# Whole-row pieces of the expert weights, and both column halves of a matrix accumulated together

## The reference

```
logits = x @ w_router + b_router;  top 4 of 32 experts, softmax over the 4
for each expert e, rows xb that chose it:
    gate = min(xb @ w_gate[e] + b_gate[e], 7)
    up   = clip(xb @ w_up[e] + b_up[e], -7, 7)
    glu  = gate * sigmoid(1.702 * gate)
    out  = ((up + 1) * glu) @ w_down[e] + b_down[e]
y[token] += weight * out
```

## Time and profile before

| what | value |
|---|---|
| time, median of 3 runs | 2386.68 us (2386.51, 2386.68, 2390.77) |
| profiled execution, first to last instruction | 2388.7 us (no other time of its own is given) |
| TensorE busy | 2262.0 us, 95% |
| VectorE busy | 1463.2 us, 61% |
| ScalarE busy | 1098.7 us, 46% |
| DMA | 493.68 MB, 207 GB/s over the span |

### The profile page before, as it was taken

How to read it: one execution, slowest core, us unless ns; L and a number is a source line. 1 busy time by engine, 2 the same in 40 slices (tenths; PEclk the granted TensorE clock), 3 DMA queues, 4 the chain that set the end, 5 groups by cost and what they waited for, 6 DMA issues and landing times. The chain is left out here.

```text
span 2388.7 us, 28681 instructions
## 1 busy us (share of the span) xinstructions
PE 2262.0 (95%) x10214; PEld 1643.8 (69%) x10215; DVE 1463.2 (61%) x1924; ACT 1098.7 (46%) x1057; POOL 89.8 (4%) x182
## 2 busy tenths in 40 slices
PE   7988999997799879999999999999999999999996
PEld 2765737774467567777777777777777777777774
DVE  1345222424100157878788888878887878788773
ACT  2241121201110037657676675765775656566552
POOL 0211202002000000000000000000000000000000
PEclk9899999986799959999999999999999999999998
DMA  8251251201524328778788787877886778678640
GB/s 307 77 176 37 71 210 71 80 1 36 196 80 141 121 78 294 263 259 300 280 298 303 267 315 277 298 247 281 291 318 234 268 251 307 228 283 315 228 158 24
DMA packets 262257, 493.68 MB, mean 207 GB/s; under 512 B 9883, under 2 KB 27484, under 8 KB 262151
## 3 DMA queue, kind: packets, MB, share of 16 engines
q1 hardware_dynamic: 260362, 490.69, 58.0%
q10 hardware_dynamic: 1840, 2.25, 0.3%
HBM read 486.47 MB, written 6.43 MB: 206 GB/s over the span
## 5 line engine op out<-in xcount | busy, mean ns | idle before, releaser
L1784 DVE TENSOR_TENSOR low<-ring,high 128x2048 fp32r<-128x2048 f32 x384 | 865.1, 2287 | 129.3 <-ACT high L1589 129.3
L1589 ACT ACTIVATE high<-ring 128x2048 fp32r<-128x2048 f32 x384 | 732.5, 1921 | 195.5 <-PE ps_moe L1666 125.6
L1663 PE MATMUL ps_moe<-high,xh 128*128 128x512 f32 x1024 | 414.2, 404 | 2.2 <-DVE xh L1789 2.2
L1666 PE MATMUL ps_moe<-low,xh 128*128 128x512 f32 x1024 | 400.8, 391 | 0.0
L1648 PE MATMUL ps_moe<-pick,work 128*128 128x128 f32 (+1 forms) x1584 | 285.4, 311 | 3.1 <-DVE pick L1751 3.1
L724 PE MATMUL ps_mix<-hT,ring 128*128 128x320 f32 x896 | 265.1, 453 | 16.0 <-ACT cbuf L641 6.7
L1648 PEld LDWEIGHTS ps_moe<-pick,work 128*128 128x128 f32 (+1 forms) x1584 | 221.1, 193 | 65.0 <-issue 3.8
L724 PEld LDWEIGHTS ps_mix<-hT,ring 128*128 128x128 f32 x896 | 175.8, 199 | 92.8 <-issue 18.3
L1663 PEld LDWEIGHTS ps_moe<-high,xh 128*128 128x128 f32 x1024 | 193.2, 189 | 57.1 <-issue 18.4
L1666 PEld LDWEIGHTS ps_moe<-low,xh 128*128 128x128 f32 x1024 | 193.5, 189 | 37.7
L1663 PE MATMUL ps_moe<-high,hh 128*128 128x512 f32 x512 | 206.7, 404 | 0.0
(11 more groups left out here) (354 smaller groups left out, 2111.9 us busy)
## 6 DMA issues: line engine op xcount, KB each, us to landing
ring<-in_w_gate SPq DMA_DIRECT2D x128, 1024.0 KB, 7.3
ring<-in_w_up SPq DMA_DIRECT2D x128, 1024.0 KB, 5.1
ring<-in_w_down SPq DMA_DIRECT2D x128, 1024.0 KB, 6.5
ring<-in_w_in SPq DMA_DIRECT2D x18, 2048.0 KB, 7.9
ring<-in_w_ada SPq DMA_DIRECT2D x12, 2048.0 KB, 8.1
states<-in_state_gdn_rec SPq DMA_DIRECT2D x8, 512.0 KB, 8.2
out_rec_sample<-states SPq DMA_DIRECT2D x8, 512.0 KB, 3.2
ring<-in_w_branch_b SPq DMA_DIRECT2D x2, 2048.0 KB, 15.8
```

The costliest lines, as they stand in the source:

```text
L1589: nc.scalar.activation(r(high[:, p % SPLIT]), raw_piece(ring, p), ACT.Copy).then_inc(high_s, 1)
L1663: nc.tensor.matmul(ps[:, bank, :], r(high_x[:, c, :]), r(hb[:, k, :]), start=c == 0, stop=False)
L1666: last = nc.tensor.matmul(ps[:, bank, :], r(high_x[:, c, :]), r(lb[:, k, :]), start=False, stop=False)
L1784: nc.vector.tensor_tensor(r(low[:, p % SPLIT]), raw_piece(ring, p), high[:, p % SPLIT], ALU.subtract).then_inc(low_s, 1)
```

## The change

A piece is now 256 whole rows of a matrix, and a partition gets two neighbouring rows, 2048 floats that lie together. A piece therefore holds two row chunks for both column halves: the even rows of the 256 and the odd ones. `half` becomes `matrix`, which accumulates both column halves in two banks, goes through four pieces, and ends with two bias matmuls in a row. Because row chunk c is now every second row, the stationary operands of `gather` and `fold_half` are read with a step of two elements (`pair_rows`), so that x and hid have their rows in the same order. TensorE's order becomes matrix 0, matrix 1, then fold (0,0), (0,1), combine 0, fold (1,0), combine 1, fold (1,1), gather, matrix 2. ScalarE and VectorE are put in a new order to match; the numbers and sizes of their instructions stay.

```diff
-            name, a, q = ("w_gate", "w_up", "w_down")[p // 4], p // 2 % 2, p % 2
-            src = t[name][0, e, QUART * P * q:QUART * P * (q + 1), HALF * a:HALF * a + HALF].rearrange("(c p) n -> p c n", p=P)
-            sp.dma_start(raw_piece(ring, p), src).then_inc(raw_full[p % RAW], 16)
+            name, q = ("w_gate", "w_up", "w_down")[p // 4], p % 4
+            src = t[name][0, e, 2 * P * q:2 * P * (q + 1), :].rearrange("(p c) n -> p (c n)", c=2)
+            sp.dma_start(raw_piece(ring, p).rearrange("p c n -> p (c n)"), src).then_inc(raw_full[p % RAW], 16)
...
ScalarE:
-                    act.wait_ge(piece_t, PIECES * i + 4 * m + 2 * a + 2)
+                    act.wait_ge(piece_t, PIECES * i + 4 * m + 4)
...
-                for p in range(3, 6):
+                for p in range(3, 7):
                     round_piece(p)
                 rows_out(0, 0)
-                for p in range(6, 8):
-                    round_piece(p)
                 rows_out(0, 1)
-                for p in range(8, 10):
+                for p in range(7, 11):
                     round_piece(p)
                 rows_out(1, 0)
...               (the two sigmoids)
-                for p in range(10, 12):
-                    round_piece(p)
                 rows_out(1, 1)
+                round_piece(11)
...
TensorE:
-                                                h2tok[0:n, tau, P * c:P * c + P], pick[0:n, tau, :],
+                                                h2tok[0:n, tau, pair_rows(c)], pick[0:n, tau, :],
...
+            def matrix(i, m, high_x, low_x, wide):
                 rows = slice(64, 128) if m == 1 else slice(0, 64)
+                for q in range(4):
+                    p = 4 * m + q
+                    pe.wait_ge(low_s, PIECES * i + p + 1)
+                    hb, lb = (x[:, p % SPLIT].rearrange("p k n -> p (k n)") for x in (high, low))
+                    for kk in range(2):
+                        c = 2 * q + kk
+                        for a in range(2):
+                            cols = slice(D * kk + HALF * a, D * kk + HALF * a + HALF)
+                            out = ps[:, 2 * m + a, :]
+                            nc.tensor.matmul(out, r(high_x[:, c, :]), r(hb[:, cols]), start=c == 0, stop=False)
+                            if wide:
+                                nc.tensor.matmul(out, r(low_x[:, c, :]), r(hb[:, cols]), start=False, stop=False)
+                            last = nc.tensor.matmul(out, r(high_x[:, c, :]), r(lb[:, cols]), start=False, stop=False)
+                    if q == 3:
+                        if m == 0:
                             pe.wait_ge(chosen_s, i + 1)
+                        for a in range(2):
+                            last = nc.tensor.matmul(ps[:, 2 * m + a, :], r(chosen[rows, :]),
+                                                    r(brow[rows, m // 2, HALF * a:HALF * a + HALF]), start=False, stop=True)
                     last.then_inc(piece_t, 1)
...
-                                            raw[:, HALF * a + P * c:HALF * a + P * c + P], fold[:], start=True, stop=True)
+                                            raw[:, pair_rows(4 * a + c)], fold[:], start=True, stop=True)
...
-                halves(n_tok, b, i, 0, 0, xh, xl)
-                halves(n_tok, b, i, 1, 1, xh, xl)
+                matrices(n_tok, b, i, 0, xh, xl)
                 if not first:
                     pe.wait_ge(put_s, i)
-                halves(n_tok, b, i, 2, 2, xh, xl)
+                matrices(n_tok, b, i, 1, xh, xl)
                 fold_half(i, 0, 0)
                 fold_half(i, 0, 1)
                 if not first:
                     combine(i - 1, 0)
                 fold_half(i, 1, 0)
-                halves(n_tok, b, i, 3, 3, xh, xl)
                 if not first:
                     combine(i - 1, 1)
                 fold_half(i, 1, 1)
...
-                halves(n_tok, b, i, 4, 4, hh, hl)
-                halves(n_tok, b, i, 5, 5, hh, hl)
+                matrices(n_tok, b, i, 2, hh, hl)
...
VectorE (left 3 to 7 and the picks before it unchanged):
                 left(8)
+                left(9)
...               (gate minima; for a = 0: product, clip, product, add_up)
-                        left(9)
+                        left(10)
...               (a = 1, then the split of hh)
-                for p in range(10, 12):
-                    left(p)
+                left(11)
...
+def pair_rows(c):
+    return slice(2 * P * (c // 2) + c % 2, 2 * P * (c // 2) + 2 * P, 2)
```

More of the change, by code:

```diff
@@ L1648, in gather @@
                         last = nc.tensor.matmul(ps[:, c // 4, CAP * (c % 4):CAP * (c % 4) + CAP],
-                                                h2tok[0:n, tau, P * c:P * c + P], pick[0:n, tau, :],
+                                                h2tok[0:n, tau, pair_rows(c)], pick[0:n, tau, :],
                                                 start=tau == 0, stop=tau == NTILE - 1)
                 last.then_inc(gath_t, 1)
-            def half(i, j, bank, high_x, low_x, wide):
-                m, a = j // 2, j % 2
+            def matrix(i, m, high_x, low_x, wide):
@@ L1669, in half @@
                             pe.wait_ge(chosen_s, i + 1)
-                        last = nc.tensor.matmul(ps[:, bank, :], r(chosen[rows, :]),
-                                                r(brow[rows, m // 2, HALF * a:HALF * a + HALF]), start=False, stop=True)
+                        for a in range(2):
+                            last = nc.tensor.matmul(ps[:, 2 * m + a, :], r(chosen[rows, :]),
+                                                    r(brow[rows, m // 2, HALF * a:HALF * a + HALF]), start=False, stop=True)
@@ L1672, in half, with matrices @@
                     last.then_inc(piece_t, 1)
-            def halves(n_tok, b, *args):
+            def matrices(n_tok, b, *args):
                 with pe.If(n_tok > CAP * b + CAP // 2):
-                    half(*args, True)
+                    matrix(*args, True)
                 with pe.Else():
-                    half(*args, False)
+                    matrix(*args, False)
             def fold_half(i, m, a):
```

## The result

The changed kernel takes 2416.0 us (median of 4 runs, 2414.8 to 2425.5) against 2387.3 before (median of 4 runs, 2386.5 to 2390.8). By the medians it is 28.8 us slower. The ratio on record is 1.0129, with a 95% interval of 1.0110 to 1.0148; the two medians alone give 1.0120. The forecast was 10 us slower. The sign and every wait were right; the size was not: the loss is nearly three times as large.

What follows compares the result with a forecast made beforehand. TensorE's order was taken to bound the expert loop. 23 narrow experts at +0.36 us, 8 wide at +0.58 and the first at -2.7 gave +10 us: 2399 us, or 2397 on the median; range 2376 to 2424.

Steps and rivals of the forecast that it cites:

- weight loads with a step of two: 48 gather and 32 fold loads an expert: strided reading costs 0; other end a whole load more each, 486 us.
- Joints: TensorE's steps into and out of the bias matmuls: one pair per matrix, -0.41 us a matrix, -1.23 an expert.
- rival B: Joints on TensorE give more than the combine takes, second bias hidden too: -19, 2368 us; chance 0.17.
- The last fold's wait: Fold (1,1) waiting for rows out (1,1), which now comes ahead of round 11: -0.40 us.
- The second combine's wait: Combine directly after fold (1,0) waits for VectorE's first add: +1.69 us narrow, +2.21 wide.
- Piece 7: TensorE waits for VectorE's `low` of the eighth piece, with no folds between pieces: +0.30 us, narrow only.
- VectorE at the gates: VectorE's gate minima start at 18.97, fold (0,1) done at about 18.5; 1.3 us of lateness still hidden.
- Loads: DMA transfers of the weight pieces: nothing in either direction, gain at most 0.8 us; slack some 2.5 us.
- The rival that had this mechanism: Strided weight loads in gather and folds pace matmuls at 0.19 instead of 0.118: +184, 2580 us; chance 0.10.
- The first expert: Narrow, without a combine: -1.23 and about half its 2.86 us wait at the last fold, -2.7 in all.

Runs made afterwards that it cites:

- e4: Changed kernel with the first bias matmul issued right after its own bank's last matmuls, ahead of the other bank's; 2464.4 us, ratio 1.0323.
- e2: Changed kernel with partitions taking rows p and 128 + p (two 4 KB runs) and stationary operands read without a step; 2404.4 us.
- e9: Kernel before with one ScalarE step moved: rows out (1,1) ahead of round 11 instead of behind it; 2372.9 us, ratio 0.9933.
- e3: Changed kernel with the four adds of the previous expert's first half moved on VectorE to right behind the gate minima; 2356.9 us.
- e8: e2 with the first combine between matrix 0 and matrix 1 and its four adds right behind the picks; 2336.0 us, ratio 0.9782.
- e1: Kernel before with only the stationary operands of gather and folds read with a step of two elements; 2403.9 us, ratio 1.0072.
- e5: Kernel before with stationary operands of gather and folds read with a step of four elements; 2793.5 us, one run.
- e6: Kernel before with stationary operands read with a step of eight elements in the gather, four in the folds; 2806.7 us, one run.

## Why the prediction was wrong

The step that failed is the term for weight loads with a step of two, which was put at nothing. Term by term:

- **Joints, -0.41 a matrix.** Right: 8.14 us against 8.13, and e4 puts them back, 0.41 in matrix 0. The second bias is not hidden (that would have given 7.90), so rival B falls.
- **The last fold's wait, -0.40.** Right: no such wait is left after, combine and fold together are 0.41 shorter in e2, and e9 gains 0.42 by this step alone.
- **The second combine's wait, +1.69 narrow.** Right in place and size: 2.50 from the fold in e2, 2.54 in the changed kernel, against 2.49. e3, which takes it away, gains 1.77 narrow and 2.29 wide. The forecast left out that the clock may fall after a long stop. That cost 1.67 us each time in e2 and e4, and nothing in the changed kernel, whose 8 wide waits had no fall behind them.
- **Piece 7, +0.30.** Right: 8.47 against 8.14, 0.33, narrow only, and e8 takes it away.
- **VectorE at the gates.** Right: late, by 0.2 us, and hidden.
- **Loads.** Right: 0.2 us of waits for DMA in all. The longer runs gave nothing.
- **Weight loads with a step of two, taken as 0.** This step failed. The forecast took the rows without a step as they stood, with the load behind the matmul, and put 0 at one end and a whole load more (486 us) at the other. The loads were not behind with room to spare: the step costs 0.31 us in a gather and about 0.05 in each of four folds, 0.51 (e1) to 0.54 us (e2) an expert, 16 to 17 us in all. That is the difference: 10 forecast and 17 make 27, measured 28.8, with an interval of 26 to 35. The prediction's own remark, that so near the fold's pace any slowing would show, was right, and the sum did not use it. The rival that had this mechanism priced it at 184 us, ten times too high, with a chance of 0.10; the ends were far apart and the value stood at one of them.
- **The first expert, -2.7.** In e2 it is 35.39 us against 39.14, -3.75. The part beyond the forecast is the clock: of the wait itself, e9 gives back 1.9 us (the forecast took half of 2.86), and the fall behind it, 1.5 us in the kernel before, was in no term. In the profiled execution of the changed kernel a longer stretch at the lower level hides this gain.

The range held the time. The forecast missed the size, by this one term.

## What to carry to other kernels

When a block of work is moved away from between two steps, write down what each later instruction waits for and which engine's order that hangs on, and move that step too: here moving four adds turned a loss of 1.2% into a gain of 1.2% (e3). A cost that is put at nothing because the work lies behind something needs the room in numbers, and where matmuls stand 0.118 us apart with a load behind each, 6 ns on each of 2560 loads are nearly the whole error. Change a layout by the variant that leaves the operands packed, if there is one; here the form with runs of 4 KB (e2) gave back just what the step had cost (0.54 us an expert, against 0.51 in e1), so giving up the runs of 8 KB lost nothing.

## What the runs showed of the hardware

- A float32 weight load of 128 columns with a step of two elements costs 6 ns more in rows of short matmuls (0.118 to 0.124 us from one fold matmul to the next, e1). With a step of four it is 0.24 us (e5), at full granted clock. A step of eight in the gather is not much worse than four (15.6 against 15.4 us, e6 and e5, both partly at the lower clock).
- Two bias matmuls of 64 rows behind each other pay one joint; a joint, in and out, costs 0.41 us in a stream of 0.227 us matmuls (e4), and a branch between matrices showed no cost of its own.
- After a stop of 2 us TensorE's granted clock fell to the lower level for 3.4 us in 4 of 8 wide experts in e2, in 5 of 8 in e4 and in none of 8 in the changed kernel, 1.67 us lost each time. After the stops of 1.4 us in the narrow experts it never did. In the first expert, after a stop of 1.7 us, the clock fell for 20 us in the profiled execution of the changed kernel and for 17 us in e4, and not at all in e2 and e3.
- A fall needs no stop: in e5, with loads that hold the matmuls 0.24 us apart, the clock fell in every gather while TensorE went on working.
